# Attention: the splits of the weight blocks get places of their own in the orders of ScalarE and VectorE

## What is computed

```
h = x + 1/2 * SwiGLU_1(RMSNorm(x))            # width 2816
u = RMSNorm(h);  proj = u @ w_in              # columns: qa 512, ka 128, va 128, qb 512, kb 512, vb 512
# rotary on q and k
# group A: 8 query heads, 2 key heads, window of 3 chunks of 64, a sink per head in the softmax
p = exp(s - m) / (sum(exp(s - m)) + exp(sink - m));   oa = p @ v
# group B: 4 heads of differential attention, causal by chunks of 64
a = softmax(s1) - lam * softmax(s2);                  ob = rmsnorm(a @ v) * 0.8
h = h + concat(oa, ob) @ w_out
h = h + 1/2 * SwiGLU_2(RMSNorm(h));   y = rmsnorm(h)
```

## Time and profile before

| | us |
|---|---|
| median of 3 runs | 1163.9 |
| lowest and highest | 1162.18 and 1164.23 |
| the profiled execution | 1163.48 |
| its span in the profile | 1161.7 |
| TensorE, VectorE, ScalarE busy in the span | 1093.8, 701.2, 477.1 |

### The profile page before, as it was taken

The page is one execution under the profiler, slowest core; times in us unless marked ns, Lnnn a source line. Parts: engine busy times, 40 slices in busy tenths (PEclk is TensorE's granted clock), DMA queues, the critical chain, the costliest instruction groups (busy, mean ns, idle before and its releaser), DMA issues.

```text
span 1161.7 us, 18954 instructions
## 1 busy us (share of the span) xinstructions
PE 1093.8 (94%) x7874; PEld 1057.8 (91%) x7874; DVE 701.2 (60%) x1046; ACT 477.1 (41%) x803; POOL 90.2 (8%) x84
## 2 busy tenths in 40 slices
PE   9989999999999999878898859999999999999995
PEld 9989999999999999766777649999999999999994
DVE  5887832588863342556676644478883248886324
ACT  6445531255553332323334533334563125555221
POOL 0000000000001122111222102200000000000011
PEclk9999999999999999889998859999999999999997
DMA  5233123222222233301011102223313222222202
GB/s 191 74 109 109 54 98 104 92 85 98 98 76 76 85 101 109 123 19 47 16 63 33 50 1 86 79 73 109 110 50 101 91 105 75 107 97 76 77 25 82
DMA packets 22660, 94.43 MB, mean 81 GB/s; under 512 B 2928, under 2 KB 6000, under 8 KB 18096
## 3 DMA queue, kind: packets, MB, share of 16 engines
q1 hardware_dynamic: 22576, 93.23, 23.8%
HBM read 88.24 MB, written 4.98 MB: 80 GB/s over the span
## 4 chain that ended last, share of the span: by engine, by line
PE 76%; DVE 14%; ACT 6%; issue 3%; POOL 0%; DVEq 0%; ACTq 0%
PE acc L609 35%; PE acc L678 33%; PE acc L801 3%; ACT w_hi L975 2%; DVE w_lo L1317 2%; PE acc L889 1%; PE acc L748 1%; DVE st L1633 1%; ACT c_hi L1053 1%; DVE comb L1431 1%; DVE st L1626 1%; ACT probs L1210 1%; DVE probs L1667 1%; ACT probs L1200 1%; DVE res L1768 1%
## 5 line engine op out<-in xcount | busy, mean ns | idle before, releaser
L1317 DVE TENSOR_TENSOR w_lo<-raw,w_hi 128x1024 fp32r<-128x1024 f32 (+3 forms) x145 | 175.8, 1212 | 266.3 <-ACT w_hi L975 265.5
L678 PE MATMUL acc<-c_hi,w_hi 128*128 128x288 f32 x952 | 282.3, 297 | 5.5 <-DVE w_lo L1317 5.5
L678 PE MATMUL acc<-c_hi,w_lo 128*128 128x288 f32 x952 | 283.4, 298 | 0.0
L678 PE MATMUL acc<-c_lo,w_hi 128*128 128x288 f32 x952 | 283.3, 298 | 0.0
L975 ACT ACTIVATE w_hi<-raw 128x1024 fp32r<-128x1024 f32 (+3 forms) x145 | 149.2, 1029 | 191.3 <-PE acc L609 173.1
L609 PE MATMUL acc<-h_hi,w_hi 128*128 128x288 f32 x1024 | 223.2, 298 | 3.9 <-DVE w_lo L1317 3.9
L609 PE MATMUL acc<-h_hi,w_lo 128*128 128x288 f32 x1024 | 222.3, 297 | 0.0
L609 PE MATMUL acc<-h_lo,w_hi 128*128 128x288 f32 x1024 | 222.0, 297 | 0.0
L678 PEld LDWEIGHTS acc<-c_hi,w_hi 128*128 128x128 f32 x952 | 179.9, 189 | 5.9 <-DVE w_lo L1317 5.9
L678 PEld LDWEIGHTS acc<-c_lo,w_hi 128*128 128x128 f32 x952 | 179.8, 189 | 0.0
L678 PEld LDWEIGHTS acc<-c_hi,w_lo 128*128 128x128 f32 x952 | 179.5, 189 | 0.0
(11 more groups left out here) (198 smaller groups left out, 1327.3 us busy)
## 6 DMA issues: line engine op xcount, KB each, us to landing
raw<-in_w1gu SPq DMA_DIRECT2D x17, 1024.0 KB, 4.9
raw<-in_w2gu SPq DMA_DIRECT2D x17, 1024.0 KB, 4.8
raw<-in_w1d SPq DMA_DIRECT2D x16, 704.0 KB, 4.0
raw<-in_w2d SPq DMA_DIRECT2D x16, 704.0 KB, 4.0
raw<-in_w_qk SPq DMA_DIRECT2D x13, 512.0 KB, 3.7
raw<-in_w1gu SPq DMA_DIRECT2D x10, 512.0 KB, 4.1
raw<-in_w2gu SPq DMA_DIRECT2D x10, 512.0 KB, 3.7
raw<-in_w_out SPq DMA_DIRECT2D x8, 512.0 KB, 3.6
```

What stands on the lines that cost most here:

```text
L678: m = nc.tensor.matmul(acc[:, banks[side(f)], 0:HALF], w_part[:, col:col + P], x_part[:, k, c, :], start=n in (P1, P5, P2) and k == 0 and ...
L1317: return nc.vector.tensor_tensor(cols, src, hi.bitcast(FP32), ALU.subtract).then_inc(split_ready, 1)
```

## The change

ScalarE and VectorE walk through lists of their own. `with_splits` copies `EVENTS` and puts an event ("W", b) into it: once step 0 of tile b has gone by, behind the next event of a given letter, N for ScalarE and S for VectorE, at the latest ahead of step 7 of the tile. For all eleven splits the letter comes before that. TensorE, GpSimd and SP are as before.

```diff
+def with_splits(behind, latest):
+
+    out, owed = [], None
+    for e in EVENTS:
+        if owed and (e[0] == "k" and (e[1] > owed[1] or e[2] == latest)):
+            out.append(owed)
+            owed = None
+        out.append(e)
+        if e[0] == "k" and e[2] == 0 and e[1] > FIRST_TILES:
+            owed = ("W", e[1])
+        elif e[0] == behind and owed:
+            out.append(owed)
+            owed = None
+    return out
+
+
+ACT_EVENTS = with_splits("N", 7)
+DVE_EVENTS = with_splits("S", 7)
...
-            for event in EVENTS:
-                if event[0] == "k" and event[2] == 1 and event[1] > FIRST_TILES:
+            for event in ACT_EVENTS:
+                if event[0] == "W":
                     hi_block(GENERIC[V_BLOCKS + event[1] + 1])
...
-            for event in EVENTS:
+            for event in DVE_EVENTS:
                 if event[0] == "k" and event[2] == KD - 1 and FIRST_TILES <= event[1] < len(TILES):
                     take_projection(event[1])
-                elif event[0] == "k" and event[2] == 1 and event[1] > FIRST_TILES:
+                elif event[0] == "W":
                     lo_block(GENERIC[V_BLOCKS + event[1] + 1])
```

## The result

| | before | changed |
|---|---|---|
| median (lowest to highest), us | 1163.0 (1162.0 to 1164.2), 4 runs | 1156.2 (1155.6 to 1156.7), 4 runs |
| ratio to before, 95% interval | | 0.9938 (0.9921 to 0.9955) |
| profiled execution, us (span) | 1163.5 (1161.7) | 1156.0 (1154.2) |

A forecast was written before the change was run, and what follows sets the result against it. Bound by TensorE, busy for 94% of the span. Gains at splits 4, 5, 8, 9, 10 and 12, less a clock fall and the costs of splits 6 and 7, took 5.4 us off 1163.5: 1158.1 us, range 1153.9 to 1162.5.

The forecast's parts named there:

- Split 4: Values product at 511.27 us: no longer behind `w_lo`, it waits for the turned probabilities' copy and starts 2.3 us earlier.
- Split 5: Chain from 527.75 us to the values product at 537.83: 3.3 us earlier, less 1.7 for a clock fall.
- Splits 8 and 9: TensorE's waits at 589.32, 596.51 and 601.06 us nearly go: gains of 0.4 and 1.4 us.
- Splits 10 and 12: Ahead of a head's norm: only gaps between TensorE's product and its copy can go, gaining 0.1 and 0.4 us.
- Splits 6 and 7: `w_lo` ahead of the outputs, near 552.67 and 573.15 us, overruns VectorE's gaps: costs of 0.45 and 0.35 us.
- The wait is still 3.6 us long, so I leave the low clock behind it as it is: At split 4, the wait ahead of the values product shortens from 5.89 us; no clock change was counted.
- the price of a fall: At split 5, low clock behind a new 3.1 us wait costs 1.7 us, 4.25 against 2.56 for the same instructions.
- The clock holds: Rival, chance 0.17: clock stays up behind split 5's 3.1 us wait, gaining 1.7 us more, 1156.4, at most to 1153.9.
- Later work swallows it: Rival, chance 0.25: VectorE's lead at splits 8 to 12 gains nothing; 1160.4 us, or 1162.1 with another clock fall.
- The copy delays the exponentials: Rival, chance 0.08: `w_hi` ahead of ScalarE's exponentials delays them at six places, up to 1.06 us each; 1166.1 us.
- Splits 11 and 13: Nothing: TensorE busy around 625 us; at 13, time freed by `w_lo` at 656.5 is taken again 3 us later.
- Outside attention: Sign: the forecast is wrong if anything outside attention changes by over 0.5 us.

The follow-up runs named there:

- the shift: The changed kernel with five products of ones by ones on TensorE right ahead of attention, all else alike: 1156.6 us, ratio 0.9944.
- The filled runs: Dummy products put in TensorE's waits: kernel before 1160.0 us, changed kernel 1148.2 us, changed kernel with VectorE's half alone 1150.3 us.

## Why the prediction held, step by step

**The chain terms were right.** Split 4: 2.3 forecast, 2.30 measured, and the wait ends with the copy, as forecast. Split 5: 3.3 and 3.32, with the wait at 531 all but gone and one of 2.99 us in its place where I had 3.1. Splits 8 and 9: 1.8 and 1.92. Splits 10 and 12: 0.1 and 0.4; 12 brought 0.39, and 10 brought 0.09: the scores behind it start at 612.12 instead of 617.85, 5.73 us earlier, where round 26 was 5.64 earlier. Splits 6 and 7: 0.45 and 0.35 forecast as costs, 0.28 and 0.19 measured. I had put the overhang of the 1.22 us subtraction over VectorE's gap in full on the path; some 0.16 us of each was absorbed. Together 7.1 forecast, 7.5 measured, or 7.6 with split 10.

**The clock terms were not.** I had one, -1.7 at split 5. The trace has four: -1.00 at split 4, -2.63 at split 5, +1.57 at round 16 and +1.48 at round 27. Two steps failed.
The first was "The wait is still 3.6 us long, so I leave the low clock behind it as it is": the clock fell, as said, but stayed low longer. Before, 0.54 over the first 4 us and 1.00 behind them; now 0.50 over the first 4 and still 0.66 over the next 3. This took 1.0 us.
The second was the price of a fall, read from one pair of pieces (4.25 and 2.56 us) that end with the maxima: low clock went on behind them to 538.5, so that the fall cost 2.6. Ahead of rounds 16 and 27 the waits were all but what they were (3.10 for 2.85, 2.30 for 2.30) and the clock behind them was better; no rule by the length of a wait gives that.
The four sum up to -0.6 and are those of one execution; the run with five dummy products ahead of attention has another set of them, and 6.9 us of gain in attention as well. Each of the four is larger than their sum. That they nearly cancel, and so that the forecast came as near as it did, is luck; the chains are not. Of the 1.5 us by which attention gave more than the forecast, 1.1 are this term and 0.4 the chains.

**The rivals.** *The clock holds* named the right doubt. In the profiled execution of the changed kernel it didn't hold behind the 2.99 us wait; with splits 4 and 5 alone, with tiles 6 and 7 back, and with the shift it did. *Later work swallows it* is refuted: splits 8 and 9 kept their 1.9 us. But a piece of it was true of the kernel before, where filled waits gave back 3.6 us to a chain. *The copy delays the exponentials* is refuted: at nine of the eleven places ScalarE, done with `w_hi`, still waits 0.28 to 2.85 us for the maxima before its next exponentials. At splits 3 and 4 these begin as the copy ends, some 0.2 us and under 0.1 us after the maxima were there; that is all there is of it. The filled runs show ScalarE's half as a gain of 1.8 us.

**Splits 11 and 13** were "nothing" in the sum, and in this kernel they are nothing. The reason I gave, that TensorE is busy there without a gap that VectorE ends, holds only at this clock. With the waits filled they are worth 3.0 us.

**Outside attention** I said that nothing would change by over 0.5 us. The changed kernel enters attention 0.6 to 0.7 us earlier, with the same instructions in the same order up to there. It is 0.8 us behind at 85 us and 0.7 ahead at 103 us, and keeps that. This too is the clock: in its trace it is low from 50.2 to 53.7 us, behind the wait of 2.12 us, and in the trace before from 84.9 to 88.3, behind one of 2.95 us that is 2.52 in the changed kernel. The other kernels here enter attention anywhere from level to 1.6 us ahead. It is no effect of the change, but my bound of 0.5 us, which had no term for the clock out there, was too small for what that part varies by. The difference between the spans, 7.5, holds it; 6.9 is what attention gave.

## What to carry to other kernels

Price a moved instruction by the chain it leaves and the chain it joins, place by place, and read the idle time of the engine that sets the end, not of the one that waits: here 22.6 us of removed waiting were 7.5 us of time. Keep falls of the clock in a sum of their own and don't decide on a variant by them; where two versions differ by a few us, fill TensorE's waits in both with products that nobody reads and compare again, since that makes visible what low clock hides. With TensorE at its full clock the chains over the other engines set more of the time, and here reordering them paid more: 10.8 us of attention for 6.9.

## What the runs showed of the hardware

- A float32 product of ones, 128 by 128 by 128, that nobody reads takes 0.235 us (13 in 3.06 us) and keeps the clock up across a wait. In the kernel with all places filled, waits of 1.3 to 4.5 us were 0.2 to 0.8 us of idle time behind 4 to 16 of them. All the places filled, with two splits put back, were worth 14.1 us of 1156.2.
- Behind waits of 2.1 to 3.1 us both clocks occur. Those behind the waits of 2.98 and 3.09 us at rounds 10 and 15 are the other way about than in the changed kernel (2.99 and 3.10) when attention starts some 0.1 us earlier, and behind the same 2.12 us at 48 to 49 us both occur with nothing changed ahead of it.
- A subtraction on VectorE, 128x1024, took 1.22 us at nine of eleven places before, and 2.23 and 1.85 us at the two where GpSimd was at work beside it (483.7 and 544.2 us). In the new order GpSimd is idle at all eleven, and the longest took 1227 ns; the forecast had taken 1.22 us for each and had not seen this. That this is GpSimd's doing is an inference from the timelines; no run here tried it alone.
